# VectorE transposes u times v of tile 0 in the last three chunks of the gated layer; memory's keys and values are copied ahead of two weight units on ScalarE

## Chip, cores and metric

One core of a Trainium2 chip runs one program of 15522 instructions. The metric is device time in microseconds (us), the median over runs of the same program.

## The reference

Two transformer blocks follow each other on x of 256 tokens by 1024 channels, all in float32. The change touches two places.

The first is the gated layer of the first block. It computes z = gelu(norm(x) W_in), splits z into u and v of 2048 channels each, normalizes v, mixes v over the 128 tokens of a chunk with one masked 128x128 matrix for each of 8 groups, adds a bias, and returns (u * v) W_out. For the last product the elementwise product u * v has to be turned, because TensorE contracts over partitions.

```
u, v = jnp.split(z, 2, axis=-1)
v = _rms_norm(v, g_sgu)
...
v = jnp.einsum('gij,bnjgc->bnigc', w, v) + b_s.T[None, None, :, :, None]
return (u * v) @ w_out
```

The second is the first feed-forward of the second block, x + 0.5 swiglu(norm(x)). Beside it the kernel prepares the keys and values of the later attention to a memory of 256 rows: k = norm(norm(mem) W_k) and v = norm(mem) W_v, 256 columns each.

## The kernel before

The program is written engine by engine: `tensor`, `scalar`, `vector`, `gpsimd` and `sync` each issue their instructions in a fixed order, and semaphores join them (`inc` marks an event, `e.wait_ge(*at(...))` waits for it). There is no planner; the order in the functions is the order of each engine's queue. The 256 tokens are two tiles of 128, called t = 0 and 1.

**Products in three passes.** A float32 product is made of three matmuls of float32r parts (`three`, lines 325 to 327): high by high, low weights by high, high by low. So every weight is split. SyncE loads a unit of 128x2048 float32 into one of three buffers `raw` (line 2182), ScalarE rounds it to the high part `whi` (line 1051), VectorE subtracts to get the low part `wlo` (line 1504). Six slots hold split units; ScalarE's `split` waits until TensorE has used the unit that was in the slot, and SyncE's load waits until VectorE has split the unit three before. Each engine splits units at fixed places in its own order (`split(n)`).

**Gated layer** (`gmlp` of each engine). The v half comes first. Then, for four chunks c of 512 channels, TensorE runs: projection of u for tile 0 into bank `GB[0]` (`u_project`, 24 matmuls of 512 columns), the mixing product of tile 0 (6 matmuls of 256 columns, bank `XB[0]`), the turn of tile 1 of the chunk before (`u_turn`, four transposes of 128x128 into bank `XB[1]`, line 331) and its output product for tile 0 (`downs`), then projection and mixing for tile 1, the turn of tile 0 of this chunk, and the output product of tile 1 of the chunk before. ScalarE makes the gelu of u into `ub` (line 1139) and, after the turn, the high part `uvThi` from bank `XB[1]` (`hi`, line 1081). VectorE's `gate` multiplies the mixed v by its gain (line 1600), adds the bias and multiplies by u in place in `ub` (line 1607), `lo` makes `uvTlo` (line 1563), and then come 2, 4, 4 and 2 splits. VectorE's order in a chunk is: gate of tile 0, low part of the other tile of the chunk before, gate of tile 1, low part of tile 0, splits.

**Feed-forward** (`ffn`). Eleven chunks of 256 hidden channels; for each, TensorE projects gate and up for tile 0 and tile 1 (24 matmuls each, banks `GB[0]` and `GB[1]`) and then multiplies the hidden values of the chunk before by `w_dn` (24 matmuls). ScalarE makes the silu (line 1166), VectorE the product with up (line 1628), and VectorE turns both tiles' hidden values at once with 16 transposes of 32 partitions by 128 elements (`turn_hid`, line 1636), block (i, j) going to block (j, i).

**Memory beside it.** In the feed-forward of the second block a hook of each engine works on memory between the chunks (`mem_keys`, a generator; `next(keys)` runs one step). After chunk 4 (`MEM_CHUNK`) TensorE projects memory's keys and values for tile 0 into `GB[0]` and tile 1 into `GB[1]`. ScalarE then copies each tile's keys to `kv` and values to `vm` (line 1081) and squares the keys (line 1078). TensorE's chunk 5 waits for `vm` of a tile before it projects into that tile's bank again. ScalarE's `beside(4)` splits two units before it takes this step of `mem_keys`; one more unit follows.

Of the kernel before, what the change touches and what calls it, by code (L numbers as in the profile page):

```python
# [18 lines left out]
MEM_CHUNK = 4  # L19
# [7 lines left out]
class Signals:  # L27
# [31 lines left out]
    def at(self, name, *key):  # L59
        return self.sem(name), 0 if self.counting else self.value[name, key]  # L60
# [77 lines left out]
def block(nc, io, out):  # L138
# [181 lines left out]
    def tensor(e):  # L320
# [98 lines left out]
        def gmlp():  # L419
            def warm(n):  # L420
                for _ in range(n):
                    e.matmul(PS[7][:, 0:128], ident[:, :], ident[:, :], start=True, stop=True)

            e.wait_ge(*at("pool", "ident"))
            warm(4)
            def turn_in(t, h):
                e.wait_ge(*at(f"x{t}{h}"))
                turn_x("g", t, h, (XB, DB[0])[t][h])

            def first_v(t, kts, last=False):  # L430
                project(("v", 0, t), GB[t], half_of(xT, t), pair, kts=kts, normed=("g", t), last=last)

            turn_in(0, 0)
            warm(8)
            pair = [take() for _ in range(4)]
            first_v(0, range(0, 2))
            turn_in(1, 0)
            first_v(0, range(2, 4))
            turn_in(0, 1)
            first_v(1, range(0, 2), True)  # L440
            turn_in(1, 1)
            first_v(1, range(2, 4), True)
            first_v(0, range(4, 8))
            first_v(1, range(4, 8), True)
            for c in range(1, 4):
                pair = [take(), take()]
                for kts in (range(0, 4), range(4, 8)) if c == 1 else (range(8),):
                    for t in range(2):
                        if kts[0] == 0 and c > 1:
                            e.wait_ge(*at("gelu", "v", c - 2, t))  # L450
                        project(("v", c, t), VB[c % 2][t], half_of(xT, t), pair, kts=kts, last=t)

            def u_project(c, t, pair):
                e.wait_ge(*at("gelu", *(("u", c - 1) if c else ("v", 2)), t))
                project(("u", c, t), GB[t], half_of(xT, t), pair, last=t)
                if c == 0:
                    e.wait_ge(*at("vlo", 3, t))
                    e.wait_ge(*at("wslo", t))
                if c or t:
                    e.wait_ge(*at("spm", *((c, 0) if t else (c - 1, 1))))  # L460
                for g in range(2):
                    vs = [a[:, 512 * c + 256 * g:512 * c + 256 * g + 256] for a in vparts[t]]
                    m = three(PS[XB[0]][:, 256 * g:256 * g + 256], [a[:, 2 * c + g, :] for a in wsp[t]], vs, True, True)
                m.then_inc(*inc("product", "mix", c, t))

            def u_turn(c, t):
                e.wait_ge(*at("uv", c, t))
                if c or t:
                    e.wait_ge(*at("uvlo", *((c, 0) if t else (c - 1, 1))))
                turn(XB[1], [ub[t][:, 128 * i:128 * i + 128] for i in range(4)], "uv", c, t)  # L470

            def downs(c, t, dn, first, last=False):
                e.wait_ge(*at("uvlo", c, t))
                for h in range(2):
                    m = down_bank(h, DB[t][h], uvT[t], dn, range(4), first, last, fresh=t == 0 and h == 0)
                    if last:
                        m.then_inc(*inc("product", "sum", "g", t, h))
                if not last:
                    m.then_inc(*inc("product", "down", "g", c, t))
                    if t:  # L480
                        used(*dn)

            for c in range(4):
                pair = [take(), take()]
                u_project(c, 0, pair)
                if c > 0:
                    u_turn(c - 1, 1)
                    dn = [take(), take()]
                    downs(c - 1, 0, dn, c == 1)
                u_project(c, 1, pair)  # L490
                u_turn(c, 0)
                if c > 0:
                    downs(c - 1, 1, dn, c == 1)
            u_turn(3, 1)
            dn = [take(), take()]
            downs(3, 0, dn, False, True)
            e.wait_ge(*at("uvlo", 3, 1))
            return sums_of_x1("g", DB[1], uvT[1], dn, range(4), False, dn)
# [537 lines left out]
        keys = mem_keys()  # L1036
# [7 lines left out]
    def scalar(e):  # L1044
# [51 lines left out]
        def gmlp():  # L1096
            e.wait_ge(*at("pool", "mhalf"))
            e.activation(stat("first use"), stat("mhalf"), ACT.Gelu)
            u0, u1 = next(nth), next(nth)
            split_part(u0, 0)  # L1100
            scaled_hi("g", 0, 0)
            split_part(u0, 1)
            split_part(u1, 0)
            split_part(u1, 1)
            scaled_hi("g", 1, 0)
            split(2)
            scaled_hi("g", 0, 1)
            for h in range(2):
                e.wait_ge(*at(f"x0{h}"))
            square_sum("g", 0, x[0][:, :])  # L1110
            scaled_hi("g", 1, 1)
            split()
            for h in range(2):
                e.wait_ge(*at(f"x1{h}"))
            e.wait_ge(*at("ssq", "g", 0))
            square_sum("g", 1, x[1][:, :])
            split()
            for c in range(4):
                for t in range(2):
                    e.wait_ge(*at("product", "v", c, t))  # L1120
                    if c == 0:
                        e.wait_ge(*at("pool", "rstd", "g", t))
                    else:
                        e.wait_ge(*at("vlo", c - 1, t))
                    e.activation(ub[t][:, :], PS[VB[c % 2][t]][:, :], ACT.Gelu, scale=stat("r", "g", t)).then_inc(*inc("gelu", "v", c, t))
                    e.wait_ge(*at("gelu", "v", c, t))
                    copy(vparts[t][0][:, 512 * c:512 * c + 512], ub[t][:, :], "vhi", c, t)
                    if c == 3 and t:
                        e.wait_ge(*at("wslo", 0))
                    e.activation(junk[:, 0:512], ub[t][:, :], ACT.Square, accum_out=stat("vss", c, t)).then_inc(*inc("vsq", c, t))  # L1130
                    if c == 3:
                        e.wait_ge(*at("wsm", t))
                        copy(flat(wsp[t][0]), junk[:, :], "wshi", t)
                split((3, 2, 2, 2)[c])

            def u_gelu(c, t):
                e.wait_ge(*at("product", "u", c, t))
                e.wait_ge(*(at("turned", "uv", c - 1, t) if c else at("vlo", 3, t)))
                e.activation(ub[t][:, :], PS[GB[t]][:, :], ACT.Gelu, scale=stat("r", "g", t)).then_inc(*inc("gelu", "u", c, t))

            def hi(c, t):
                e.wait_ge(*at("turned", "uv", c, t))
                if c > 1:
                    e.wait_ge(*at("product", "down", "g", c - 1, t))
                elif c == 1:
                    e.wait_ge(*at("product", "down", "g", 0, t))
                copy(flat(uvT[t][0]), PS[XB[1]][:, :], "uvhi", c, t)

            for c in range(4):
                u_gelu(c, 0)  # L1150
                if c:
                    hi(c - 1, 1)
                u_gelu(c, 1)
                hi(c, 0)
                split((2, 4, 4, 2)[c])
            hi(3, 1)
            split(2)

# [320 lines left out]
        keys = mem_keys()  # L1479

        def beside(c):
            if c == MEM_CHUNK:
                split(2)
            if c in (2, 3, MEM_CHUNK):
                next(keys)
            if c == MEM_CHUNK + 4:
                e.wait_ge(*at("clamped"))
                a = ang[:, :, :, :].rearrange("p a b c -> p (a b c)")
                e.activation(a, a, ACT.Sin).then_inc(*inc("sin"))
# [7 lines left out]
    def vector(e):  # L1497
# [67 lines left out]
        def gmlp():  # L1565
# [29 lines left out]
            def gate(c, t):  # L1595
# [11 lines left out]
                    v = e.scalar_tensor_tensor(out=ub[t][:, cs], in0=m[:, cs], scalar=bsp[:, 2 * c + g:2 * c + g + 1], in1=ub[t][:, cs], op0=ALU.add, op1=ALU.mult)  # L1607
                v.then_inc(*inc("uv", c, t))

            def lo(c, t):  # L1610
                evac_lo([flat(a) for a in uvT[t]], PS[XB[1]][:, :], "uvhi", "uvlo", c, t)

            for c in range(4):
                gate(c, 0)
                if c == 0:
                    split()
                else:
                    lo(c - 1, 1)
                gate(c, 1)
                lo(c, 0)  # L1620
                split((2, 4, 4, 2)[c])
# [731 lines left out]
```

## Time and profile before

| | us |
|---|---|
| runs, median of 3 | 1170.08 |
| runs, lowest and highest | 1169.73, 1170.96 |
| the profiled execution, its own time | 1169.77 |
| its span, first to last instruction | 1167.9 |
| TensorE busy | 1155.3 (99%) |
| VectorE busy | 890.6 (76%) |
| ScalarE busy | 600.7 (51%) |
| GpSimd busy | 54.6 (5%) |

The profile is one execution, recorded by the hardware. Times are from the start of the span. In it PE is TensorE's matmuls, PEld its weight loads, DVE VectorE, ACT ScalarE, POOL GpSimd, SP SyncE. A row of the timeline gives start and duration in us, engine, source line, operation, output and inputs with shape, how many instructions it merges, and in brackets how long the engine stood idle before it and what released it. Names of tiles come without their buffer number, with a prefix for their region (`g_` gated layer, `f_` feed-forward, `m_` memory). Matmuls are pipelined: a row of 0.39 us may be followed 0.23 us later by the next.

### The profile page before, as it was taken

Reading aid. Unit: us, or ns where it says so; the run is one execution under the profiler, and the core shown is the slowest. Engines: PE = TensorE matmul, PEld = TensorE weight load, DVE = VectorE, ACT = ScalarE, POOL = GpSimd, SP = SyncE. Lnnn points to the kernel's source line nnn. Section 1 sums busy time; section 2 is a strip of 40 time slices with the busy share of each in tenths; the row PEclk is TensorE's granted clock in tenths of the full one; section 3 lists DMA queues with packets and bytes.
Section 4 is the critical chain, followed back from the end, with each engine's and each line's share of the span. In section 5 each row is a group of like instructions: output and inputs, shape, how many; then the busy total and the mean of one; then the engine's idle time right before and its main releaser. Section 6 shows DMA issues by size and latency. Waiting matters only on the chain.

```text
span 1167.9 us, 15522 instructions
## 1 busy us (share of the span) xinstructions
PE 1155.3 (99%) x5969; PEld 965.9 (83%) x5969; DVE 890.6 (76%) x1598; ACT 600.7 (51%) x797; POOL 54.6 (5%) x109
## 2 busy tenths in 40 slices
PE   9999999999999999999999999999999999999998
PEld 7888888888889988888888887888898787888887
DVE  6666577987857768798886996888568777979874
ACT  7744454544445555454344464444467867545441
POOL 1100010000000000000001300000110002000000
PEclk9999999999999999999999999999999999999999
DMA  7744536555444443665453645465355142555530
GB/s 289 288 154 158 211 113 245 220 216 194 172 176 178 148 145 145 234 234 215 170 192 131 259 176 212 181 233 196 133 208 189 38 145 72 201 232 216 216 144 36
DMA packets 34689, 213.56 MB, mean 183 GB/s; under 512 B 4665, under 2 KB 6841, under 8 KB 10041
## 3 DMA queue, kind: packets, MB, share of 16 engines
q1 hardware_dynamic: 34617, 212.59, 49.0%
q8 instruction: 47, 0.77, 0.3%
q14 instruction: 25, 0.20, 0.0%
HBM read 211.53 MB, written 1.05 MB: 182 GB/s over the span
## 4 chain that ended last, share of the span: by engine, by line
PE 95%; DVE 2%; ACT 1%; DMA 1%; issue 1%; SPq 0%; POOL 0%; DVEq 0%; POOLq 0%
PE ps L325 30%; PE ps L326 29%; PE ps L327 29%; PE ps L331 3%; PE ps L762 1%; DVE wlo L1504 1%; DMA raw<-in_w_v 1%; PE ps L813 1%; PE ps L635 1%; PE ps L790 0%; PE ps L615 0%; DVE tmp L1523 0%; PE ps L737 0%; ACT xThi L1072 0%; PE ps L823 0%
## 5 line engine op out<-in xcount | busy, mean ns | idle before, releaser
L1504 DVE TENSOR_TENSOR wlo<-raw,whi 128x2048 fp32r<-128x2048 f32 (+2 forms) x196 | 433.1, 2232 | 45.1 <-ACT whi L1051 45.1
L1051 ACT ACTIVATE whi<-raw 128x2048 fp32r<-128x2048 f32 (+2 forms) x196 | 364.9, 1868 | 152.4 <-DMA raw<-in_w_gu 80.3
L325 PE MATMUL ps<-whi,xThi 128*128 128x512 f32 (+2 forms) x960 | 373.6, 389 | 4.3 <-issue 2.8
L327 PE MATMUL ps<-whi,xTlo 128*128 128x512 f32 (+2 forms) x960 | 371.0, 386 | 0.0
L326 PE MATMUL ps<-wlo,xThi 128*128 128x512 f32 (+2 forms) x960 | 370.8, 386 | 0.0
L325 PEld LDWEIGHTS ps<-whi,xThi 128*128 128x128 f32 x960 | 180.4, 188 | 42.9 <-issue 4.4
L327 PEld LDWEIGHTS ps<-whi,xTlo 128*128 128x128 f32 x960 | 180.4, 188 | 36.4
L326 PEld LDWEIGHTS ps<-wlo,xThi 128*128 128x128 f32 x960 | 180.5, 188 | 35.0
L1636 DVE STREAM_TRANSPOSE f_sil<-f_hid 32x128 f32<-32x128 f32 x640 | 193.8, 303 | 13.1 <-DVE f_hid L1628 0.9
L325 PE MATMUL ps<-whi,f_hThi 128*128 128x512 f32 x352 | 138.3, 393 | 0.0
L327 PE MATMUL ps<-whi,f_hTlo 128*128 128x512 f32 x352 | 137.3, 390 | 0.0
L326 PE MATMUL ps<-wlo,f_hThi 128*128 128x512 f32 x352 | 137.2, 390 | 0.0
L1166 ACT ACTIVATE f_sil<-ps,stats 128x256 f32<-128x256 f32 x88 | 40.5, 469 | 176.0 <-PE ps L327 175.1
L1628 DVE SCALAR_TENSOR_TENSOR f_hid<-ps,stats,f_sil 128x256 f32<-128x256 f32 x88 | 42.3, 481 | 68.3 <-ACT f_sil L1166 68.2
L327 PEld LDWEIGHTS ps<-whi,f_hTlo 128*128 128x128 f32 x352 | 66.1, 188 | 13.7
L325 PEld LDWEIGHTS ps<-whi,f_hThi 128*128 128x128 f32 x352 | 66.2, 188 | 13.3
L326 PEld LDWEIGHTS ps<-wlo,f_hThi 128*128 128x128 f32 x352 | 66.2, 188 | 13.2
L1081 ACT ACTIVATE f_hThi<-f_sil 128x256 fp32r<-128x256 f32 x80 | 28.9, 409 | 48.4 <-DVE f_sil L1636 48.4
L1563 DVE TENSOR_TENSOR f_hTlo<-f_sil,f_hThi 128x256 fp32r<-128x256 f32 x80 | 30.5, 422 | 20.6 <-ACT f_hThi L1081 20.6
L2089 POOL TENSOR_SCALAR stats<-stats 128x1 f32<-128x1 f32 (+3 forms) x27 | 14.2, 524 | 647.9 <-ACT junk L1075 556.6
L1072 ACT ACTIVATE xThi<-tmp 128x512 fp32r<-128x512 f32 x32 | 19.9, 629 | 38.5 <-DVE tmp L1523 38.3
L325 PE MATMUL ps<-xThi,whi 128*128 128x256 f32 x128 | 37.0, 289 | 0.5 <-DVE wlo L1504 0.5
(289 smaller groups left out, 1160.9 us busy)
## 6 DMA issues: line engine op xcount, KB each, us to landing
raw<-in_w_gu SPq DMA_DIRECT2D x88, 1024.0 KB, 4.8
raw<-in_w_dn SPq DMA_DIRECT2D x44, 1024.0 KB, 5.2
raw<-in_w_u SPq DMA_DIRECT2D x8, 1024.0 KB, 6.3
raw<-in_w_ao SPq DMA_DIRECT2D x8, 1024.0 KB, 5.2
raw<-in_w_v SPq DMA_DIRECT2D x6, 1024.0 KB, 5.0
raw<-in_w_bv SPq DMA_DIRECT2D x4, 1024.0 KB, 4.9
raw<-in_w_bk SPq DMA_DIRECT2D x4, 1024.0 KB, 4.7
raw<-in_w_bq SPq DMA_DIRECT2D x4, 1024.0 KB, 4.9
```

The lines of the kernel that those rows point to most:

```text
L325: e.matmul(ps, a[0], b[0], start=start, stop=False)
L326: e.matmul(ps, a[0], b[1], start=False, stop=False)
L327: return e.matmul(ps, a[1], b[0], start=False, stop=stop)
L331: m = e.transpose(PS[bank][:, 128 * i:128 * i + 128], s, ident[:, :])
L1051: e.activation(dst[:, cs], raw_cols(i, cs), ACT.Copy).then_inc(*inc("whi", i, p))
L1072: e.activation(parts[0][:, 4 * h:4 * h + 4, 128 * t:128 * t + 128], tmp[h][:, :, :], ACT.Copy).then_inc(*inc("xhi", S, t, h))
L1081: e.activation(dst, src, ACT.Copy, scale=scale).then_inc(*inc(name, *key))
L1166: e.activation(sil[t][:, :], PS[GB[t]][:, 0:256], ACT.Silu, scale=stat("r", S, t)).then_inc(*inc("silu", S, c, t))
L1504: e.tensor_tensor(lo[:, cs], raw_cols(i, cs), hi[:, cs].bitcast(F32), ALU.subtract).then_inc(*inc("wlo", i, p))
L1563: e.tensor_tensor(dst[1], ps, dst[0].bitcast(F32), ALU.subtract).then_inc(*inc(name, *key))
L1628: e.scalar_tensor_tensor(out=hid[t][:, :], in0=PS[GB[t]][:, 256:512], scalar=stat("r", S, t), in1=sil[t][:, :], op0=ALU.mult, op1=ALU.mult ...
L1636: m = e.transpose(both_sil[32 * j:32 * j + 32, :, 32 * i:32 * i + 32], both_hid[32 * i:32 * i + 32, :, 32 * j:32 * j + 32])
```

## The change

VectorE gets a `u_turn` of its own: in chunks 1, 2 and 3 it turns u times v of tile 0 with 16 transposes of 32 partitions from `ub[0]` into the first 512 columns of `junk`, block (i, j) to block (j, i), and marks `uvturn`. It stands after the low part of the other tile and before the gate of tile 1. TensorE turns tile 0 only in chunk 0; tile 1 is turned by TensorE as before. ScalarE's `hi` and VectorE's `lo` read `junk` for those three chunks, and the next gelu into `ub[0]` waits for `uvturn`. On TensorE the turn of tile 1 waits for the low part of tile 1 of the chunk before, since bank `XB[1]` no longer holds tile 0 from chunk 1 on. In ScalarE's `beside`, the step of `mem_keys` comes before the two splits, not after.

```diff
--- before.py
+++ after.py
@@ -464,9 +464,10 @@
                 m.then_inc(*inc("product", "mix", c, t))
 
             def u_turn(c, t):
+
                 e.wait_ge(*at("uv", c, t))
-                if c or t:
-                    e.wait_ge(*at("uvlo", *((c, 0) if t else (c - 1, 1))))
+                if t:
+                    e.wait_ge(*(at("uvlo", c - 1, 1) if c else at("uvlo", 0, 0)))
                 turn(XB[1], [ub[t][:, 128 * i:128 * i + 128] for i in range(4)], "uv", c, t)
 
             def downs(c, t, dn, first, last=False):
@@ -488,7 +489,8 @@
                     dn = [take(), take()]
                     downs(c - 1, 0, dn, c == 1)
                 u_project(c, 1, pair)
-                u_turn(c, 0)
+                if c == 0:
+                    u_turn(c, 0)
                 if c > 0:
                     downs(c - 1, 1, dn, c == 1)
             u_turn(3, 1)
@@ -1135,16 +1137,16 @@
 
             def u_gelu(c, t):
                 e.wait_ge(*at("product", "u", c, t))
-                e.wait_ge(*(at("turned", "uv", c - 1, t) if c else at("vlo", 3, t)))
+                e.wait_ge(*(at("turned" if t or c == 1 else "uvturn", "uv", c - 1, t) if c else at("vlo", 3, t)))
                 e.activation(ub[t][:, :], PS[GB[t]][:, :], ACT.Gelu, scale=stat("r", "g", t)).then_inc(*inc("gelu", "u", c, t))
 
             def hi(c, t):
-                e.wait_ge(*at("turned", "uv", c, t))
+                e.wait_ge(*at("turned" if t or c == 0 else "uvturn", "uv", c, t))
                 if c > 1:
                     e.wait_ge(*at("product", "down", "g", c - 1, t))
                 elif c == 1:
                     e.wait_ge(*at("product", "down", "g", 0, t))
-                copy(flat(uvT[t][0]), PS[XB[1]][:, :], "uvhi", c, t)
+                copy(flat(uvT[t][0]), PS[XB[1]][:, :] if t or c == 0 else junk[:, 0:512], "uvhi", c, t)
 
             for c in range(4):
                 u_gelu(c, 0)
@@ -1479,10 +1481,10 @@
         keys = mem_keys()
 
         def beside(c):
+            if c in (2, 3, MEM_CHUNK):
+                next(keys)
             if c == MEM_CHUNK:
                 split(2)
-            if c in (2, 3, MEM_CHUNK):
-                next(keys)
             if c == MEM_CHUNK + 4:
                 e.wait_ge(*at("clamped"))
                 a = ang[:, :, :, :].rearrange("p a b c -> p (a b c)")
@@ -1607,8 +1609,17 @@
                     v = e.scalar_tensor_tensor(out=ub[t][:, cs], in0=m[:, cs], scalar=bsp[:, 2 * c + g:2 * c + g + 1], in1=ub[t][:, cs], op0=ALU.add, op1=ALU.mult)
                 v.then_inc(*inc("uv", c, t))
 
+            def u_turn(c):
+
+                a, b = (v.rearrange("p (k n) -> p k n", k=4) for v in (ub[0][:, :], junk[:, 0:512]))
+                e.wait_ge(*at("uv", c, 0))
+                for i in range(4):
+                    for j in range(4):
+                        m = e.transpose(b[32 * j:32 * j + 32, :, 32 * i:32 * i + 32], a[32 * i:32 * i + 32, :, 32 * j:32 * j + 32])
+                m.then_inc(*inc("uvturn", "uv", c, 0))
+
             def lo(c, t):
-                evac_lo([flat(a) for a in uvT[t]], PS[XB[1]][:, :], "uvhi", "uvlo", c, t)
+                evac_lo([flat(a) for a in uvT[t]], PS[XB[1]][:, :] if t or c == 0 else junk[:, 0:512], "uvhi", "uvlo", c, t)
 
             for c in range(4):
                 gate(c, 0)
@@ -1616,6 +1627,8 @@
                     split()
                 else:
                     lo(c - 1, 1)
+                if c:
+                    u_turn(c)
                 gate(c, 1)
                 lo(c, 0)
                 split((2, 4, 4, 2)[c])
```

## Rows read from the trace of the kernel before

**Rows 1.** The page, engines: busy time, share of the span, instructions
```profile
PE 1155.3 (99%) x5969; PEld 965.9 (83%) x5969; DVE 890.6 (76%) x1598; ACT 600.7 (51%) x797; POOL 54.6 (5%) x109
```

**Rows 2.** The page, the chain that ended last, by engine
```profile
PE 95%; DVE 2%; ACT 1%; DMA 1%; issue 1%; SPq 0%; POOL 0%; DVEq 0%; POOLq 0%
```

**Rows 3.** Waits of TensorE over the whole span: total us, times, longest
```profile
PE ps L325 <- issue: 2.8, 1, 2.8
```

**Rows 4.** Timeline of TensorE, feed-forward of the second block: start us, us
```profile
712.53 0.39 PE L327 MATMUL ps<-whi,m_mTlo 128*128 128x512 f32 x1
...
717.98 0.39 PE L327 MATMUL ps<-whi,m_mTlo 128*128 128x512 f32 x1
721.14 0.47 PE L325 MATMUL ps<-whi,xThi 128*128 128x512 f32 x1 [2.77 <-issue]
721.44 0.40 PE L326 MATMUL ps<-wlo,xThi 128*128 128x512 f32 x1
```

**Rows 5.** Timeline of ScalarE in the same stretch
```profile
715.68 1.92 ACT L1051 ACTIVATE whi<-raw 128x2048 fp32r<-128x2048 f32 x1 [5.11 <-PE ps L327]
718.40 1.91 ACT L1051 ACTIVATE whi<-raw 128x2048 fp32r<-128x2048 f32 x1 [0.80 <-PE ps L327]
720.22 0.46 ACT L1081 ACTIVATE m_kv<-ps,stats 128x256 f32<-128x256 f32 x1
720.57 0.47 ACT L1081 ACTIVATE m_vm<-ps,stats 128x256 f32<-128x256 f32 x1
...
722.25 1.93 ACT L1051 ACTIVATE whi<-raw 128x2048 fp32r<-128x2048 f32 x1
726.90 0.47 ACT L1166 ACTIVATE f_sil<-ps,stats 128x256 f32<-128x256 f32 x1 [2.71 <-PE ps L327]
```

**Rows 6.** Timeline of VectorE in the same stretch
```profile
710.97 4.49 DVE L1504 TENSOR_TENSOR wlo<-raw,whi 128x2048 fp32r<-128x2048 f32 x2
717.63 2.29 DVE L1504 TENSOR_TENSOR wlo<-raw,whi 128x2048 fp32r<-128x2048 f32 x1 [2.17 <-ACT whi L1051]
```

**Rows 7.** Issues of the weight loads: count, KB each, us to landing
```profile
raw<-in_w_gu SPq DMA_DIRECT2D x88, 1024.0 KB, 4.8
```

**Rows 8.** Timeline of TensorE, gated layer: mixing product without and with a turn behind
```profile
60.53 0.28 PE L327 MATMUL ps<-g_vhi,g_wslo 128*128 128x256 f32 x1
...
60.88 0.40 PE L326 MATMUL ps<-wlo,xThi 128*128 128x512 f32 x1
...
85.39 0.28 PE L327 MATMUL ps<-g_vhi,g_wslo 128*128 128x256 f32 x1
85.52 0.60 PE L331 MATMUL ps<-ident,g_ub 128*128 128x128 f32 x4
...
86.19 0.39 PE L326 MATMUL ps<-wlo,g_uvThi 128*128 128x512 f32 x1
```

**Rows 9.** Timeline of VectorE, gated layer
```profile
76.23 0.68 DVE L1563 TENSOR_TENSOR g_uvTlo<-ps,g_uvThi 128x512 fp32r<-128x512 f32 x1
85.72 0.69 DVE L1600 TENSOR_TENSOR tmp<-ps,g_gs 128x512 f32<-128x512 f32 x1 [8.80 <-PE ps L327]
...
109.84 0.69 DVE L1600 TENSOR_TENSOR tmp<-ps,g_gs 128x512 f32<-128x512 f32 x1 [7.67 <-PE ps L327]
...
133.97 0.69 DVE L1600 TENSOR_TENSOR tmp<-ps,g_gs 128x512 f32<-128x512 f32 x1 [7.69 <-PE ps L327]
...
136.84 4.49 DVE L1504 TENSOR_TENSOR wlo<-raw,whi 128x2048 fp32r<-128x2048 f32 x2 [0.66 <-ACT whi L1051]
```

**Rows 10.** Timeline of VectorE, feed-forward: the same sixteen transposes
```profile
165.13 5.05 DVE L1636 STREAM_TRANSPOSE f_sil<-f_hid 32x128 f32<-32x128 f32 x16
```

**Rows 11.** Instructions of two tiles of the gated layer: ns min/median/max
```profile
L1081 ACT ACTIVATE g_uvThi<-ps x8: 598/598/602, 67.5 to 140.3; 128x512 fp32r<-128x512 f32 x8
...
L1081 ACT ACTIVATE g_vhi<-g_ub x8: 631/632/637, 22.3 to 55.9; 128x512 fp32r<-128x512 f32 x8
```

**Rows 12.** Timeline of TensorE, output product of the last chunk, tile 0
```profile
141.51 0.40 PE L325 MATMUL ps<-whi,g_uvThi 128*128 128x512 f32 x1
```


## The prediction

> **What bounds the kernel now.** First the page's engines: TensorE is busy 1155.3 us of a span of 1167.9 [rows 1], and the chain that ended last runs over it for 95% [rows 2]. So a microsecond of its work that goes is a microsecond of the time, unless something else is late just behind; and an engine with idle time, VectorE at 76% or ScalarE at 51%, can take work for nothing where the idle time lies in the right place. Next the waits of TensorE: there is one long one, 2.8 us, put down to "issue", meaning that the profile shows no releaser [rows 3]. The timeline places it: the 48 matmuls of memory's key and value projection (with `m_mThi` and `m_mTlo` in the rows) go on to the one that starts at 717.98, and the next matmul, the gate-up projection of chunk 5, tile 0, starts at 721.14 [rows 4].
>
> What ends this gap is read from the code and ScalarE's timeline together. That gate-up projection writes bank `GB[0]`, which holds memory's projection of tile 0 until ScalarE has copied keys and values out, and TensorE waits for `vm` 0. ScalarE copies that at 720.57 for 0.47 us, so to 721.04, 0.10 us before TensorE starts [rows 5]. The product of tile 0 ended at 712.53 + 0.39 = 712.92 [rows 4], 7.3 us before the copies began at 720.22: between lie two high parts of weights, at 715.68 and 718.40, each of which waited for TensorE (5.11 and 0.80 us) [rows 5]. They wait for slots that the very projection of tile 1 sets free. So the copies stood behind two units that could not start yet.
>
> In the gated layer I read TensorE around a turn, then VectorE's idle time. A mixing product followed at once by a 512-column product gives 0.35 us from its last matmul to the second matmul behind (60.53 to 60.88); with a turn of four transposes between, 0.80 us (85.39 to 86.19) [rows 8]. VectorE meanwhile is idle 8.80, 7.67 and 7.69 us ahead of the gate of tile 1 in chunks 1, 2 and 3 [rows 9].
>
> **The change part by part.** *The three turns removed from TensorE* (chunks 1 to 3, tile 0). Each is worth 0.80 - 0.35 = 0.45 us, three 1.35 us. The ends: nothing, if a wait fills the place, and 3 x 0.60 = 1.8 us, the busy time of the row. I take 1.35, which is a distance between starts in this very stage. Behind the mixing product TensorE goes straight to the output product of tile 1 of the chunk before, whose low part VectorE finished long ago (76.23 + 0.68 = 76.91 in chunk 1, against 85.5) [rows 8, 9].
>
> *Sixteen 32-row transposes on VectorE, three times.* The feed-forward layer does the same shape, 32 x 128 float32, in 5.05 us for sixteen [rows 10]: 15.15 us in all. Each group stands behind the low part of the other tile and ahead of the gate of tile 1, which is where VectorE is idle. In chunk 1 it runs from 76.9 to 82.0, and the gate starts at 85.72. In chunk 3 the mixing product comes 0.90 us earlier, by two turns already gone, so the idle time is 7.69 - 0.90 = 6.8 us, still 1.7 us more than the transposes take. Chunk 2 has 7.67 - 0.45 = 7.2. So the cost is nothing, with VectorE's idle time as the cover; what would be queued behind a longer group is the gate, the low part of tile 0 and the splits of the next weights, two to four units, on which SyncE's next loads wait.
>
> Here a rule speaks against the change. The row of a group says 5.05 us on VectorE where TensorE's turn costs 0.45 [rows 8, 10]. The Trainium skill, page "VectorE: DVE Perf Modes", section "Rules for kernel authors", says to transpose 128x128 on TensorE if the result may lie in PSUM, and it may here. By that rule each move is a loss; taken engine by engine the rows agree, and by the sum on the path they don't, because TensorE is the engine without idle time. Its result is the third rival.
>
> *The copies of tile 0.* ScalarE's high part now reads `junk` in SBUF, not a PSUM bank. The nearest rows are 598 ns from PSUM and 632 ns from SBUF for 128x512 [rows 11]: 0.03 us more, three times, before the weight splits, where ScalarE waits on TensorE and loads anyway; and it no longer waits for the turn behind its gelu. Cost nothing. The low part and the waits on `uvturn` move to earlier events. Cost nothing.
>
> *The memory copies ahead of two units.* ScalarE now waits for memory's projection first. Tile 0's copies run as soon as the product is there, from about 713.0, three operations in half of 722.25 - 720.22, so 1.0 us: `vm` 0 is there 4 us before TensorE asks. Then TensorE runs on without a gap. From 717.98 to 721.44 are 3.46 us; two steps undisturbed are 2 x (717.98 - 712.53)/24 = 0.45 us [rows 4]. The gain is 3.01 us; the idle time of the row alone, 2.77, is the lower end. `vm` 1 is ready at 718.4 + 1.0 = 719.4, and tile 1 asks for it at 718.2 + 5.45 = 723.7.
>
> What becomes later? The first two units go from 715.68 and 718.40 to about 719.5 and 721.3, the third from 722.25 to 723.2 [rows 5]. The silu of chunk 5, tile 0, could start at 726.90 - 3.01 = 723.9 and now starts at 725.1 behind them. Its product is needed at TensorE's chunk 6, three groups of 24 matmuls after 718.2, so at 734.6: covered by 9 us. VectorE's low part of the first unit moves from 717.63 to 721.4 and ends at 723.7, used at 734.6 too. The units of chunk 5 itself were split at 710.97 and before, and do not move [rows 6]. SyncE's load behind the first unit is issued at 723.7, not 719.9, and lands 4.8 us later [rows 7], at 728.5, before ScalarE's turn for it (after the silu of tile 1, at 729.3). No DMA is added.
>
> **Sum.** 3.01 + 1.35 = 4.36 us. The profiled execution took 1169.77 us, of which 1.87 lie outside its span, so 1165.4; the median of the three runs, 1170.08, stands 0.31 above it, so 1165.7. A change of under 0.2%, 2.3 us, could not be told from none here.
>
> **The rivals.** *Only the memory part counts*: the turns' 1.35 us are given back, at the entry to the next layer or where TensorE next waits for VectorE. For it: chunk 3's cover is thin by 1.7 us, and a chain tied to loads would not move forward with TensorE. Against: TensorE's other waits are short. 1170.08 - 3.01 = 1167.1.
>
> *Only the turns count*: another wait takes the gap's place, because ScalarE's queue now stands before the memory product while three units pile up behind. It would have to show by chunk 6 and be worth 3 us; I found 9 us of cover. 1170.08 - 1.35 = 1168.7.
>
> *VectorE becomes the bound in the gated layer*, the side of slower. Were its transposes on the path whole, the change would cost 3 x (5.05 - 0.45) = 13.8 us, less the 3.01: 1180.9. That is also the time by the rule of the Trainium skill's page named above. It decides from the point where the cover ends: 6.8 us in chunk 3, plus the margin of the unit split next, whose low part ends at about 136.84 + 2.24 = 139.1 and is first used at 141.51 [rows 9, 12], 2.4 us. So a group would have to take over 9.2 us against 5.05 in the row.
>
> *The change doesn't do what it says*: the gap was not the copy's and stays, and the turns are given back: 1170.1. The 0.10 us between copy and start speak against it.
>
> **How the numbers follow.** Chances: the forecast 0.77, memory alone 0.09, turns alone 0.08, neither 0.03, VectorE the bound 0.03. The range goes from 1164.9 (turns at 1.8 us, and 0.35 us for the spread of the runs below their median) to 1167.3 (memory alone, at 2.77); this leaves out the last three cases, 0.14, and takes in both ends of the two unknown terms. Faster by over 0.2%: forecast and memory alone, 0.86. Within: turns alone and neither, 0.11. Slower: 0.03.
>
> **What would show it.** TensorE's waits should have no line of 2.8 us, and the first gate-up matmul should stand 0.23 us behind memory's last. ScalarE should copy `vm` 0 some 7 us earlier, ahead of the two units. The turns of `g_ub` should be 20 matmuls, not 32, and VectorE should show three groups of about 5.05 us ending before the gate of tile 1, with idle time still ahead of it. I am wrong if a gate waits for nothing but VectorE's own transposes, if a wait for `wlo` appears on TensorE between 85 and 150 us or around the chunk 6 and 7 of that feed-forward layer, or if the entry to the layer behind the gated one grows.

## The result, and the profile after

The changed kernel took 1165.16 us in the median of six runs (1164.74 to 1165.67), the kernel before 1170.52 in six runs beside and ahead of it (1169.25 to 1171.85). The ratio is 0.9949, with a 95% interval of 0.9939 to 0.9959: 4.8 to 7.1 us of 1170.08, and 6.0 in the middle, which is 1164.1 on the first scale. The profiled execution took 1165.28 us, with a span of 1163.4. So faster, as forecast; but the traces differ by 4.5 us of span (1167.9 to 1163.4), close to the sum's 4.36, while the runs differ by 5.4 (the medians) to 6.0 (the ratio). The median of 1165.16 itself lies in the range of 1164.9 to 1167.3, but the six runs of before beside it stand 0.44 above the three that the range was worked out from, and the middle of the ratio lies below its low end. That difference is what the experiments are about.

Each step first, in the profile after. Its line numbers stand two higher than before in the functions of ScalarE and 2 to 13 higher in those of VectorE. The page's engines, as in [rows 1]:

```profile
PE 1153.6 (99%) x5957; PEld 964.3 (83%) x5957; DVE 904.7 (78%) x1646; ACT 600.2 (52%) x797; POOL 53.9 (5%) x109
```

TensorE has 12 matmuls fewer and VectorE 48 instructions and 14.1 us more. TensorE's waits, the two longest of the list, as in [rows 3]:

```profile
PE ps L422 <- POOL ident L2113: 1.8, 1, 1.8
PE ps L325 <- DVE wlo L1506: 1.4, 4, 0.5
```

The line of 2.8 us is gone. What stands in its place on the timeline of TensorE, and then the copies on that of ScalarE, as in [rows 4, 5]:

```profile
716.53 0.39 PE L327 MATMUL ps<-whi,m_mTlo 128*128 128x512 f32 x1
716.75 0.39 PE L325 MATMUL ps<-whi,xThi 128*128 128x512 f32 x1
716.98 0.39 PE L326 MATMUL ps<-wlo,xThi 128*128 128x512 f32 x1
```

```profile
711.89 0.47 ACT L1083 ACTIVATE m_vm<-ps,stats 128x256 f32<-128x256 f32 x1
...
717.33 0.47 ACT L1083 ACTIVATE m_vm<-ps,stats 128x256 f32<-128x256 f32 x1
717.68 0.42 ACT L1080 ACTIVATE junk<-m_kv 128x256 f32<-128x256 f32 x1
717.99 5.52 ACT L1053 ACTIVATE whi<-raw 128x2048 fp32r<-128x2048 f32 x3
723.40 0.47 ACT L1168 ACTIVATE f_sil<-ps,stats 128x256 f32<-128x256 f32 x1
```

From memory's last matmul to the second one behind are 0.45 us, where 3.46 had been: 3.01 us, the term of the sum to the last digit. Values of tile 0 are copied by 712.36, 4.4 us before TensorE asks; the three units follow in one piece behind the copies of tile 1, and the silu behind them at 723.40.

The gated layer: TensorE around the place of the turn, then VectorE's first group, the gates of tile 1 and the last split of chunk 1 with the gate of tile 0 behind it, then the instructions of `ub` and of the high part, as in [rows 8 to 11]:

```profile
85.29 0.28 PE L327 MATMUL ps<-g_vhi,g_wslo 128*128 128x256 f32 x1
85.41 0.40 PE L325 MATMUL ps<-whi,g_uvThi 128*128 128x512 f32 x1
85.64 0.40 PE L326 MATMUL ps<-wlo,g_uvThi 128*128 128x512 f32 x1
```

```profile
76.71 5.04 DVE L1618 STREAM_TRANSPOSE junk<-g_ub 32x128 f32<-32x128 f32 x16
85.61 0.69 DVE L1602 TENSOR_TENSOR tmp<-ps,g_gs 128x512 f32<-128x512 f32 x1 [3.86 <-PE ps L327]
...
97.27 2.29 DVE L1506 TENSOR_TENSOR wlo<-raw,whi 128x2048 fp32r<-128x2048 f32 x1 [1.95 <-ACT whi L1053]
99.48 0.69 DVE L1602 TENSOR_TENSOR tmp<-ps,g_gs 128x512 f32<-128x512 f32 x1
...
109.30 0.69 DVE L1602 TENSOR_TENSOR tmp<-ps,g_gs 128x512 f32<-128x512 f32 x1 [2.66 <-PE ps L327]
...
132.98 0.69 DVE L1602 TENSOR_TENSOR tmp<-ps,g_gs 128x512 f32<-128x512 f32 x1 [2.88 <-PE ps L327]
```

```profile
L1618 DVE STREAM_TRANSPOSE junk<-g_ub x48: 289/303/307, 76.7 to 129.8; 32x128 f32<-32x128 f32 x48
...
L331 PE MATMUL ps<-ident,g_ub x20: 270/272/273, 66.7 to 138.6; 128*128 128x128 f32 x20
...
L1083 ACT ACTIVATE g_uvThi<-junk x3: 623/623/625, 85.5 to 132.9; 128x512 fp32r<-128x512 f32 x3
```

A mixing product is followed in 0.35 us by the second matmul behind it, as it was without a turn. A group takes 5.04 us, and every gate of tile 1 still waits for TensorE, with 2.66 to 3.86 us of idle time left. The high part from `junk` takes 623 ns, 25 more than from PSUM.

### The profile page after: what moved, and what is told of

Its sections match the earlier page's. It is cut to its first block, busy times and chain, and to the rows that moved or that the text cites. A ratio compares the mean times of both kernels' runs of the same rounds, so it can differ in the third digit from the quotient of the medians.

```text
span 1163.4 us, 15543 instructions
## 1 busy us (share of the span) xinstructions
PE 1153.6 (99%) x5957; PEld 964.3 (83%) x5957; DVE 904.7 (78%) x1646; ACT 600.2 (52%) x797; POOL 53.9 (5%) x109
## 4 chain that ended last, share of the span: by engine, by line
PE 95%; DVE 2%; ACT 1%; DMA 1%; SPq 0%; issue 0%; POOL 0%; DVEq 0%; POOLq 0%
PE ps L325 30%; PE ps L327 29%; PE ps L326 29%; PE ps L331 3%; PE ps L764 1%; DVE wlo L1506 1%; DMA raw<-in_w_v 1%; PE ps L815 1%; PE ps L637 1%; PE ps L792 0%; PE ps L617 0%; DVE tmp L1525 0%; PE ps L739 0%; ACT xThi L1074 0%; PE ps L825 0%
```

## The experiments

Nine experiments, two of them repeats without an edit. The first four ran on one chip and share 22 runs of the kernel before (median 1171.05); the next four on a second chip (21 runs, 1171.14); the last on a third (13 runs, 1171.20).

**The kernel before, against itself.** No edit.

> The kernel before, unchanged, timed against itself. Two theories of why the runs gained 5.4 to 6 us where the traces differ by 4.5. Theory A (the sum): the change is worth 4.36 us, the rest is the spread of the runs of before, 1169.25 to 1171.85. Theory B (more than the trace): the kernel before loses another 1 to 1.5 us in many of its runs, at a place that the change takes away, so that its profiled execution was a lucky one. Both expect a ratio of 1.000 here. A expects single runs to lie as far apart in this copy as in the runs beside it, 2 to 3 us, and the copy's median to differ from theirs by up to 1 us. The span of this profile against 1167.9 tells how far two executions of one program stand apart.

Measured: 1171.28 us (1169.55 to 1171.75), ratio 1.0002 (0.9993 to 1.0010). Its profiled execution has a span of 1169.4, 1.5 us more than the profile before; by luck it shows where the time goes. The timeline of TensorE behind the gap, and the busy time and granted clock in slices of it (the columns are in the first line; the clock is the number ahead of the last two):

```profile
718.00 0.39 PE L327 MATMUL ps<-whi,m_mTlo 128*128 128x512 f32 x1
721.16 0.76 PE L325 MATMUL ps<-whi,xThi 128*128 128x512 f32 x1 [2.77 <-issue]
721.72 0.63 PE L326 MATMUL ps<-wlo,xThi 128*128 128x512 f32 x1
722.15 0.63 PE L327 MATMUL ps<-whi,xTlo 128*128 128x512 f32 x1
...
723.85 0.51 PE L325 MATMUL ps<-whi,xThi 128*128 128x512 f32 x1
724.20 0.40 PE L326 MATMUL ps<-wlo,xThi 128*128 128x512 f32 x1
```

```profile
core 0: us, PE busy (x) PEld busy (x) DVE busy (x) ACT busy (x) POOL busy (x), PEclk, DMA share, GB/s
...
721.00:722.00 1.00, 0.84 (x2) 0.78 (x3) 0.00 (x0) 1.00 (x5) 0.00 (x0) 0.50 0.48 147
722.00:723.00 1.00, 1.00 (x3) 0.71 (x3) 0.00 (x0) 1.00 (x3) 0.00 (x0) 0.50 0.95 401
723.00:724.00 1.00, 1.00 (x4) 0.80 (x3) 0.00 (x0) 1.00 (x1) 0.00 (x0) 0.50 0.95 401
724.00:725.00 1.00, 1.00 (x6) 0.82 (x5) 0.00 (x0) 0.19 (x1) 0.00 (x0) 0.95 0.12 49
```

The gap is the same 2.77 us. But after it TensorE runs at a granted clock of 0.50, the lower of its two levels (1.2 GHz), and a matmul follows the last after 0.43 us instead of 0.23; from 724 on the slice shows 0.95, and the clock is back at 2.4 GHz. The same slices of the profile before:

```profile
721.00:722.00 1.00, 0.86 (x4) 0.76 (x5) 0.00 (x0) 1.00 (x5) 0.00 (x0) 1.00 0.42 131
722.00:723.00 1.00, 1.00 (x6) 0.83 (x5) 0.00 (x0) 1.00 (x3) 0.00 (x0) 1.00 0.93 393
```

So seven matmuls took 724.20 - 721.16 = 3.04 us. At full clock the same seven take 1.7 us: 0.30 from 721.14 to 721.44 [rows 4], and six steps of 0.23. The difference, 1.35, is most of the 1.5 us between the spans. Every run lists its mean granted clock. Over the 67 runs of this program, those beside the other experiments included, 22 have 1.000, with a median of 1169.78 us (1169.12 to 1170.37); 45 have 0.997 to 0.999, with a median of 1171.36 (1169.78 to 1173.66), 1.58 us more. The execution that the prediction was made from, 1169.77 us at 1.000, is not among the 67 but is like the 22. The mean clock is a rough sign, not a proof for each run: only one of the 67 was traced. An execution can stand at 0.999 by its last 2 us alone, when TensorE has nothing left to do (0.55 from 1162 to 1164 us in the profile of the changed kernel run again, and 1.00 in the 720s), and two of the 45 (1169.78, 1170.38) are about as short as the 22.

**The memory order alone.**

```diff
+            if c in (2, 3, MEM_CHUNK):
+                next(keys)
             if c == MEM_CHUNK:
                 split(2)
-            if c in (2, 3, MEM_CHUNK):
-                next(keys)
```

> Only the order on ScalarE is changed; TensorE turns tile 0 in all chunks as before. Theory A: 3.0 us, ratio 0.9974, the span 3.0 shorter, the row of 2.77 us gone from TensorE's waits. Theory B, if the further loss sits at the memory gap: 4 to 4.6 us, ratio 0.9961 to 0.9966. The rival that another wait takes the gap's place: no gain, and a new wait of TensorE by chunk 6 or 7.

Measured: 1166.81 us (1166.53 to 1167.48), ratio 0.9969 (0.9957 to 0.9980), span 1164.7, no wait of TensorE over 1.8 us. The span is 3.2 us shorter than that of before. The runs are 4.2 us below the median of those beside them, and lie within 1 us of each other, where theirs spread over 3.3. The medians speak for theory B at the memory gap: 3.0 us against the 22 runs at full clock, 4.6 against the 45 others. The ratio, 0.9969, lies between A's 0.9974 and B's 0.9966, and its interval takes in both, so it doesn't decide alone.

**The turns alone.** The changed kernel with ScalarE's order put back as it was (the edit above, reversed).

> Only the turns of tile 0 are moved to VectorE; ScalarE's order is as before. Theory A: 1.35 us, ratio 0.9988, the memory gap of 2.77 us stays. Theory B, if the further loss sits at the turns: 2.3 to 2.9 us, ratio 0.9975 to 0.9980. The rival that the turns are given back: ratio 1.000, with a new wait between 140 us and the next layer. By the rule that TensorE is the place for a transpose: 13.8 us longer, ratio 1.0118.

Measured: 1169.79 us (1168.38 to 1170.66), ratio 0.9992 (0.9983 to 1.0001); the wait of 2.8 us is there. In like executions it is theory A: the span of 1166.5, at a clock of 1.000, is 1.4 below that of before, and the two runs of eleven at a mean clock of 1.000 took 1168.38 and 1168.43, against 1169.78 for the 22 of before. The other nine (0.998 and 0.999) have a median of 1169.90, against 1171.36 for the 45. Since the gap is left in, so is its spread, and by the runs alone the turns could not be told from no change.

**The changed kernel again.** No edit.

> The changed kernel once more, on the same chip as the three others. Theory A: the sum of the two halves, 4.36 us, ratio 0.9963, 0.9953 to 0.9973 with the spread of the runs. Theory B: 0.9949 again, and more than the two halves' own traces add up to.

Measured: 1165.11 us (1165.04 to 1165.55), ratio 0.9956 (0.9943 to 0.9968), span 1163.5. The median is 5.9 us below that beside it. The traces of the halves add up: 3.2 + 1.4 = 4.6 us of span, against 4.4 to 4.5 for the whole. The ratio, 0.9956, lies between A's 0.9963 and B's 0.9949 and decides nothing. That what the runs gain beyond the traces is the clock is tested by the next two.

**The gap filled.** The kernel before, with ten small products of the identity on TensorE where it waits; the compiler makes twenty matmuls of them. They add work whose result nobody reads.

```diff
                     if hook and c == MEM_CHUNK + 1:
+                        for _ in range(10 if t == 0 else 0):
+                            e.matmul(PS[XB[0]][:, 0:128], ident[:, :], ident[:, :], start=True, stop=True)
                         e.wait_ge(*at("vm", t))
```

> The kernel before, with ten small matmuls of the identity on TensorE in the gap ahead of chunk 5, into a bank that nobody reads; the copies keep their place. Theory C, formed from the copy of the kernel before: its 2.77 us of idle TensorE are followed, in 21 of 33 runs, by a stretch at the lower clock (granted 0.50 from 721 to 724 us in the profiled one) that costs 1.4 to 2 us more; the profiled execution of before was one of the other 12. C expects that filling the gap keeps the 3.0 us of waiting but takes the clock's loss from all runs: median 1169.4 to 1170.0, all runs within 1 us of each other, granted clock 1.00 in the 720s. The rival (B without the clock: the runs of before differ by loads or by chips) expects runs as far apart as before's, 1169.4 to 1172.7.

Measured: 1169.70 us (1169.31 to 1170.72), ratio 0.9990 (0.9981 to 0.9999). TensorE's timeline and a slice with the clock:

```profile
717.48 0.39 PE L327 MATMUL ps<-whi,m_mTlo 128*128 128x512 f32 x1
717.71 2.39 PE L532 MATMUL ps<-ident 128*128 128x128 f32 x20
720.63 0.50 PE L325 MATMUL ps<-whi,xThi 128*128 128x512 f32 x1 [0.53 <-ACT m_vm L1083]
```

```profile
721.00:722.00 1.00, 1.00 (x6) 0.82 (x5) 0.00 (x0) 1.00 (x4) 0.00 (x0) 1.00 0.88 344
```

With 0.53 us idle in the place of 2.77 no run has a mean clock under 0.999, and the profiled one, at 0.999, has 1.00 in the 720s. The median is that of the 22 runs of before at full clock (1169.78), though the copies are as late as ever: useless work beats waiting by 1.4 us in the medians. Here the row also names the copy of `vm` as the releaser, which [rows 3] had as "issue". Three of eleven runs (1170.35 to 1170.72) lie higher at a clock of 1.000, so the expected 1 us was exceeded; what they lost I can't say.

**A gap by another wait.** The changed kernel, copies ahead, with TensorE made to wait for a weight unit.

```diff
                     if hook and c == MEM_CHUNK + 1:
+                        if t == 0:
+                            e.wait_ge(*at("whi", 127, 0))
                         e.wait_ge(*at("vm", t))
```

> The changed kernel, with a wait of TensorE for a weight unit's high part put ahead of chunk 5, tile 0, so that a gap of about 3.0 us comes back by another cause, with the copies ahead as in the change. Theory C: 1165.1 + 3.1 = 1168.2 in the runs without the clock's fall and 1169.6 to 1170.3 in those with it, both kinds present, median about 1169.5. The rival that the spread belongs to the copies or to ScalarE's order: 1168.2 in all runs.

Measured: 1169.66 us (1168.51 to 1170.64), ratio 0.9987 (0.9978 to 0.9996). Four runs at a clock of 1.000 took 1168.51 to 1168.86; seven at 0.998 and 0.999 took 1169.40 to 1170.64. The profile is of the second kind; TensorE's timeline and a slice with the clock:

```profile
716.59 0.39 PE L327 MATMUL ps<-whi,m_mTlo 128*128 128x512 f32 x1
720.06 0.47 PE L325 MATMUL ps<-whi,xThi 128*128 128x512 f32 x1 [3.08 <-issue]
...
721.40 0.63 PE L327 MATMUL ps<-whi,xTlo 128*128 128x512 f32 x1
```

```profile
722.00:723.00 1.00, 1.00 (x4) 0.81 (x3) 0.28 (x1) 1.00 (x1) 0.00 (x0) 0.50 0.00 0
```

Copies in the good order, a gap with another cause, and the clock falls in most runs again. It is behind TensorE's idle time that the clock falls, in some executions, whatever ends that time. Here the first matmuls still ran at full clock, and the fall came a microsecond later.

**One unit ahead.** The changed kernel, with one unit split ahead of the copies and one behind.

```diff
             if c == MEM_CHUNK:
-                split(2)
+                split(1)
             if c in (2, 3, MEM_CHUNK):
                 next(keys)
+            if c == MEM_CHUNK:
+                split(1)
```

> The changed kernel with one of the two units split ahead of the copies and one behind. The unit waits for its slot until about 714.2 and ends at 716.1 in the changed kernel's times, so keys and values of tile 0 are copied by 716.9, 0.2 us after TensorE could go on at 716.7. Both theories: 0.2 to 0.4 us longer than the changed kernel, 1165.4; C: a gap this short does not touch the clock, all runs within 1 us.

Measured: 1165.40 us (1165.24 to 1166.58), ratio 0.9957 (0.9945 to 0.9970), all five runs at a clock of 1.000. The copy of `vm` ends at 716.58, and TensorE starts 0.10 us later (TensorE's timeline, then ScalarE's):

```profile
716.24 0.39 PE L327 MATMUL ps<-whi,m_mTlo 128*128 128x512 f32 x1
716.68 0.47 PE L325 MATMUL ps<-whi,xThi 128*128 128x512 f32 x1
```

```profile
716.12 0.46 ACT L1083 ACTIVATE m_vm<-ps,stats 128x256 f32<-128x256 f32 x1
```

So nearly all of the gap was the second unit, whose slot comes free only with TensorE's last memory matmuls. One run of five lies 1.3 us above the lowest.

**Two and three groups of transposes.** The changed kernel, with the sixteen transposes done once or twice more into an unused half of `junk`, ahead of the real ones. This asks how thick the cover is. With three groups:

```diff
+                spare = junk[:, 512:1024].rearrange("p (k n) -> p k n", k=4)
+                for again in range(2):
+                    for i in range(4):
+                        for j in range(4):
+                            m = e.transpose(spare[32 * j:32 * j + 32, :, 32 * i:32 * i + 32], a[32 * i:32 * i + 32, :, 32 * j:32 * j + 32])
+                    m.then_inc(*inc("uvagain", c, again))
+                    e.wait_ge(*at("uvagain", c, again))
```

> The changed kernel with three groups of sixteen transposes per chunk instead of one (the two added go to an unused part of the same buffer): 15.1 us on VectorE where the cover is 8.9, 7.7 and 7.9 us, so the gate of tile 1 comes 6.2 to 7.4 us late in each chunk. By the prediction's margins (a group decides from 9.2 us in the last chunk, 10.5 and 12.1 in the others) TensorE loses 5.9 + 4.6 + 3.0 = 13.5 us at most, 1178.6; a delay that one chunk hands to the next is counted twice in this sum, so 6 to 13.5. The clock may add to it where TensorE then stands still. The rival, that the cover is only VectorE's idle time with no margin behind it: 3 x 6.8 = 20 us, 1185. The rival that VectorE never bounds TensorE here: 1165.2.

> The changed kernel with two groups of sixteen transposes per chunk: 10.1 us on VectorE where the cover is 8.9, 7.7 and 7.9 us, so the gate of tile 1 is 1.2 to 2.4 us late in each chunk. By the prediction's margins (9.2, 10.5 and 12.1 us before TensorE waits) only the last chunk loses, 0.9 us at most: 1165.1 to 1166.0, clock 1.00. The rival from the three-fold groups, that nearly all of a delay reaches TensorE in each chunk: 1.2 + 2.4 + 2.2 = 5.8 us, 1171, with waits for the low parts of weights in TensorE's list.

Measured: three groups 1184.64 us (1184.16 to 1184.95), ratio 1.0119 (1.0105 to 1.0133); two groups 1169.42 us (1168.67 to 1170.13), ratio 0.9985 (0.9975 to 0.9994). Against the changed kernel's 1165.11 this is 19.5 us and 4.3 us. TensorE's waits with three groups, and a slice with its clock:

```profile
PE ps L325 <- DVE wlo L1506: 11.7, 6, 7.1
PE ps L331 <- DVE g_ub L1609: 4.5, 1, 4.5
```

```profile
125.00:130.00 5.00, 2.23 (x5) 1.83 (x6) 4.74 (x4) 3.99 (x3) 0.00 (x0) 0.60 0.27 49
```

The new wait of TensorE with two groups, a slice with its clock, and then VectorE: the second group of chunk 1, the gate of tile 1 of each chunk, and between the first two the last split with the gate of tile 0; then that unit on ScalarE:

```profile
PE ps L331 <- DVE g_ub L1609: 1.7, 1, 1.7
```

```profile
140.00:145.00 5.00, 3.90 (x12) 2.65 (x13) 4.71 (x6) 5.00 (x5) 0.00 (x0) 0.71 0.00 0
```

```profile
82.04 5.05 DVE L1625 STREAM_TRANSPOSE junk<-g_ub 32x128 f32<-32x128 f32 x16
87.12 0.69 DVE L1602 TENSOR_TENSOR tmp<-ps,g_gs 128x512 f32<-128x512 f32 x1
...
98.80 2.29 DVE L1506 TENSOR_TENSOR wlo<-raw,whi 128x2048 fp32r<-128x2048 f32 x1 [2.52 <-ACT whi L1053]
101.01 0.68 DVE L1602 TENSOR_TENSOR tmp<-ps,g_gs 128x512 f32<-128x512 f32 x1
...
113.27 0.69 DVE L1602 TENSOR_TENSOR tmp<-ps,g_gs 128x512 f32<-128x512 f32 x1
...
139.43 0.69 DVE L1602 TENSOR_TENSOR tmp<-ps,g_gs 128x512 f32<-128x512 f32 x1
```

```profile
96.85 1.92 ACT L1053 ACTIVATE whi<-raw 128x2048 fp32r<-128x2048 f32 x1 [3.61 <-DMA raw<-in_w_u]
```

The expectation of 0 to 0.9 us was wrong. Against the profile after the gates of tile 1 start 1.5, 4.0 and 6.5 us late: the lateness grows from chunk to chunk. That is close to the running sum of what a second group needs beyond the idle time left in the profile after (3.86, 2.66 and 2.88 us): 1.2, 3.6 and 5.8. I had taken each chunk's margin by itself. But a late gate makes the high part and the splits behind it late, these the load of the last unit, and this unit the next chunk's first gate: ScalarE waits 3.61 us for the load, VectorE's low part of it starts at 98.80 instead of 97.27, and the gate of tile 0 at 101.01 instead of 99.48. So the next group starts late by what the last one left. Of 6.5 us TensorE loses 4.3 in the medians, so some margin behind the last gate is there, but once and not in each chunk. The profiled execution is the longest of the ten (1170.13); in it TensorE waits 1.74 us for the last gate, and behind that the clock falls, to 0.71 over the slice. Eight of the ten runs list 1.000, so in most of them little of the loss can be the clock's.

The other expectation, 13.5 us at most, fell for the same reason and for one more: TensorE's idle time brings the clock down here too (0.60 in the slice), and the waits of 16.2 us are not the whole loss. The recorded rival without any margin, 20 us, comes nearest for three groups (19.5, with the clock's loss in it); its counterpart for two, 5.8 us, is too much.

## Why the prediction was right, and where it was wrong

**The turns**: right in place and size. 0.45 us each, the span 1.4 us shorter with the turns alone, against 1.35.

**The transposes on VectorE at no cost**: right. 5.04 us a group, 3.9, 2.7 and 2.9 us of cover left; the prediction had 3.7 in chunk 1 and 1.7 in chunk 3. There it let TensorE's mixing product come earlier and VectorE's own work stay; but that came earlier too (the gate of tile 0 at 122.94 us, not 124.08), and the cover did not shrink. The rival that VectorE becomes the bound, 13.8 us longer, is borne out by no run: the turns alone come out at 0.9992. A price appears where the cover is spent: three groups cost 19.5 us. The Trainium skill, page "VectorE: DVE Perf Modes", section "Rules for kernel authors", says to transpose 128x128 on TensorE where PSUM will do. The traces don't bear that out here, where TensorE is busy for 99% of the span.

**The margin behind the cover**, 9.2 us a group: wrong. A group of 10.1 us costs 4.3 us, not 0.9 at most, because lateness is handed from chunk to chunk. The chance of 0.03 stood on a margin thinner than I thought, though 5.04 us is still well inside the cover of 7.7 us and more.

**The copies ahead**: the mechanism was right, and in the traces to the hundredth, 3.01 us from memory's last matmul to the second behind it; nothing later replaced it. **The step that failed is the size of the sum's term for this gap.** I priced it by idle time alone, "The gain is 3.01 us", with 2.77 as the lower end, from an execution in which the clock stayed at 1.00 behind the gap. By the mean clock 45 of 67 runs are not like it, and those take 1.58 us more. So the order of memory alone gains 3.0 us against the runs at full clock and 4.6 against the others (1169.78 and 1171.36 to 1166.81), and the whole change 4.6 and 6.2 (to 1165.16). Where the clock stays up the sum held: worked out from the profiled execution of before it gave 1165.4, and the profiled one of after took 1165.28. What it left out is the clock's loss behind the gap, 1.4 us in the one trace of before that has it and 1.6 in the medians, which goes with the gap and which the median of many runs of before contains. I had the sign of it in hand: the runs of before spread over 1.2 us, and I used that as noise, 0.35 us at the low end, instead of asking what in the kernel makes it. That is why the range ended at 1164.9.

The Trainium skill, page "TensorE: Matmul & The Clock Gate", section "Why this matters for your kernels", advises against long idle gaps between bursts of matmuls, to avoid that the throughput drops. This gap is shorter than those that the page warns of, and the clock fell all the same: in one of the two traces of the kernel before, and by the mean clocks in about two runs of three. I had left it out because the one profile showed a clock of 1.00.

**What stays open**: why the clock falls in some executions and not in others of the same program, with a gap of 2.77 us in both profiles; what the seven of the 45 runs at a mean clock of 0.997 lost, which took 1172.30 to 1173.66 and of which none was traced; and the 0.7 to 1.3 us by which single runs of the filled gap and of the one unit ahead exceed the rest at a full clock. No run beat the changed kernel.

## What to carry to other kernels

An idle time of the engine that sets the end can cost more than it lasts: look at the granted clock behind each gap, and in more than one execution, before it is priced. When a program's single runs differ by more than those of its neighbours, take that for a property of the kernel and list the runs by their mean clock; here it separated, roughly, two kinds of execution of one program. Cover has to be counted around the whole loop: a spare microsecond in each stage is no spare at all where a late stage hands its lateness on.

## What was not expected of the hardware

An idle time of 2.77 us on TensorE, after 700 us in which the engine had hardly stood still, was followed by a granted clock of 0.50 from 721 to 724 us in one execution and 1.00 in another. In the copy of before the clock was down when TensorE began again; in the gap by another wait it fell a microsecond after work had resumed. With twenty small matmuls in the gap, leaving 0.53 us idle, no run of eleven had a mean clock under 0.999. The length of the gap does not settle it in these traces: with three groups a wait of 3.00 us ahead of 96.69 us was followed by 1.00, with two groups one of 1.74 us ahead of 141.09 by 0.50 from 143 to 145.
